# Two moves of panel splits past copies and scalings in a one-core hybrid block on Trainium2

## The reference, cut to what matters

```
proj = h @ w_in                          # all branches' inputs, panels of 256 columns
o_sb  = stick_breaking_attention(q, k, v)              # 8 heads of 64
o_nsa = gate0 * attend(q, compressed keys)             # 15 blocks of 32 tokens, stride 16
      + gate1 * attend(q, selected keys) + gate2 * attend(q, window keys)
o_hg  = hgrn2_recurrence(silu(hg_q), log f, 1 - f, hg_i)   # 4 heads of 128, then a norm and a gate
m = sigmoid(g0) * (o_sb @ w_sb) + sigmoid(g1) * (o_nsa @ w_nsa) + sigmoid(g2) * (o_hg @ w_hg)
x = x + m @ w_out
```

## Time and profile before

| | |
|---|---|
| three runs | 1978.54, 1979.7 (median), 1980.26 us |
| profiled execution | 1978.61 us, span 1976.9 us |
| busy | TensorE 91%, VectorE 67%, ScalarE 41%, GpSimd 21% of the span |
| mean granted TensorE clock | 0.967 of full speed (full is 2.4 GHz, half is 1.2 GHz) |

### The profile page before, as it was taken

One profiled execution on the slowest core, in us unless ns is written; L12 is line 12 of the kernel. 1 busy time (PEld: TensorE's weight loads), 2 busy tenths in 40 slices (PEclk: granted clock), 3 DMA queues, 4 the chain that ended last, 5 costly groups with the idle time before them and its releaser, 6 DMA issues.

```text
span 1976.9 us, 28258 instructions
## 1 busy us (share of the span) xinstructions
PE 1802.3 (91%) x9902; PEld 1375.9 (70%) x9902; DVE 1315.5 (67%) x2522; ACT 812.9 (41%) x1375; POOL 414.7 (21%) x535
## 2 busy tenths in 40 slices
PE   7999899987877787878989999999999999999998
PEld 7988798632333333323378889988889888888887
DVE  5567656867777777777665566765565655776555
ACT  4466343222223212222254444454455544665443
POOL 4000000565456545565310000000000000010000
PEclk9999899998989899998999999999999999999999
DMA  9425374999999999999966554646655656435552
GB/s 243 131 86 150 87 189 141 392 422 422 422 422 422 421 421 422 422 422 422 421 212 199 188 194 160 207 166 191 191 171 181 194 191 211 150 121 171 187 188 98
DMA packets 224244, 496.67 MB, mean 251 GB/s; under 512 B 21653, under 2 KB 170278, under 8 KB 191398
## 3 DMA queue, kind: packets, MB, share of 16 engines
q1 hardware_dynamic: 181264, 221.36, 35.6%
q0 software_dynamic: 38224, 273.04, 33.5%
q10 hardware_dynamic: 4678, 1.21, 0.3%
HBM read 494.53 MB, written 1.05 MB: 251 GB/s over the span
## 4 chain that ended last, share of the span: by engine, by line
PE 67%; DMA 13%; DVE 8%; issue 4%; POOL 3%; ACT 3%; DVEq 0%; POOLq 0%; ACTq 0%
PE ps L2257 39%; PE acc L2257 26%; DMA rows_x<-in_peer_uv,idx_now 6%; DMA arena<-in_peer_uv,idx_now 6%; DVE lo L1440 1%; DMA rows_lo<-in_peer_uv,idx_now 1%; POOL rows L747 1%; ACT hi L817 1%; DVE x L2063 1%; DVE spare_lo L1957 1%; POOL rows_lo L747 1%; POOL rstd L655 0%; ACT xboth L1152 0%; ACT spare_hi L1158 0%; POOL idx_now L740 0%
## 5 line engine op out<-in xcount | busy, mean ns | idle before, releaser
L1440 DVE TENSOR_TENSOR lo<-raw,hi 128x2048 fp32r<-128x2048 f32 x198 | 451.3, 2282 | 193.8 <-ACT hi L817 193.8
L2257 PE MATMUL ps<-xboth,hi 128*128 128x512 f32 (+2 forms) x2400 | 537.0, 344 | 2.1 <-DVE xboth L1461 2.1
L2257 PEld LDWEIGHTS ps<-xboth,hi 128*128 128x128 f32 (+1 forms) x2400 | 409.2, 191 | 47.0 <-issue 4.5
L817 ACT ACTIVATE hi<-raw 128x2048 fp32r<-128x2048 f32 x198 | 376.3, 1902 | 16.3 <-PE acc L2257 9.0
L2257 PE MATMUL ps<-xboth,lo 128*128 128x256 f32 x1840 | 338.3, 283 | 0.0
L2257 PEld LDWEIGHTS ps<-xboth,lo 128*128 128x128 f32 x1840 | 283.0, 191 | 12.6
L650 POOL TENSOR_SCALAR ss<-ss 128x1 f32<-128x1 f32 x26 | 8.9, 342 | 937.8 <-ACT arena L1220 826.1
L2257 PE MATMUL acc<-arena,diag 128*128 128x512 f32 x384 | 175.5, 602 | 8.2 <-ACT diag L1128 7.5
L2257 PE MATMUL acc<-rows,diag 128*128 128x512 f32 x192 | 113.1, 751 | 74.1 <-ACT diag L1128 62.5
L2257 PEld LDWEIGHTS acc<-arena,diag 128*128 128x128 f32 x384 | 72.8, 192 | 105.0 <-issue 85.8
L2257 PEld LDWEIGHTS acc<-rows,diag 128*128 128x128 f32 x192 | 45.1, 243 | 141.2 <-issue 128.1
(11 more groups left out here) (429 smaller groups left out, 2976.5 us busy)
## 6 DMA issues: line engine op xcount, KB each, us to landing
raw<-in_w_ffn_gate SPq DMA_DIRECT2D x44, 1024.0 KB, 5.3
raw<-in_w_ffn_down SPq DMA_DIRECT2D x44, 1024.0 KB, 5.1
raw<-in_w_ffn_up SPq DMA_DIRECT2D x41, 1024.0 KB, 5.3
raw<-in_w_in SPq DMA_DIRECT2D x29, 1024.0 KB, 5.5
raw<-in_w_conv_in SPq DMA_DIRECT2D x11, 1024.0 KB, 5.2
raw<-in_w_kv SPq DMA_DIRECT2D x6, 1024.0 KB, 5.4
raw<-in_w_out SPq DMA_DIRECT2D x4, 1024.0 KB, 5.3
raw<-in_w_conv_out SPq DMA_DIRECT2D x4, 1024.0 KB, 6.7
```

The source lines that it names most:

```text
L817: nc.scalar.activation(hi[s][:, 0:WORDS[p]], raw[s][:, 0:WORDS[p]], ACT.Copy).then_inc(hi_done, 1)
L1440: v.tensor_tensor(lo[s][:, 0:WORDS[p]], raw[s][:, 0:WORDS[p]], hi[s][:, 0:WORDS[p]].bitcast(F32), ALU.subtract).then_inc(lo_done, 1)
L2257: return nc.tensor.matmul(out, l, r, start=first, stop=last)
```

## The change

Two moves; no instruction is added or removed. In compressed attention the split of panel p + 3 = 16 + 2i goes from the end of pair i into pair i + 1 (there it is p + 1), behind that pair's scaling, for i = 0 to 2. VectorE's low halves follow in the same way. In the recurrence ScalarE's two splits of each round go ahead of the two score copies; VectorE's order there stays.

More of the change, by code:

```diff
@@ L995, in nsa_pair @@
                 p = h0 + 1 + 2 * i
+                if i:
+                    split(p + 1)
                 split(p + 2)
@@ L1006, in nsa_pair @@
                     nsa_exp(2 * i + 3, 1)
-                    split(p + 3)
                     nsa_out(i)
@@ L1031, in hg_pair @@
                     gate_evac(m0 + 2)
+                split(m0 + 4 + 2 * j)
+                split(m0 + 5 + 2 * j)
                 for a in range(2):
@@ L1035, in hg_pair @@
                     nc.scalar.activation(large_a[a], ACC[:, 3, 0:3 * P], ACT.Copy).then_inc(h_cross, 1)
-                split(m0 + 4 + 2 * j)
                 if not j:
                     gate_evac(m0 + 3)
-                split(m0 + 5 + 2 * j)
                 for a in range(2):
```

## The result

The changed kernel took 1964.4 us (median of 6 runs, 1962.9 to 1966.1) against 1979.0 (1977.6 to 1980.3, 6 runs): ratio 0.9927, 95% interval 0.9914 to 0.994, 14.6 us less.

The account below looks back on a forecast made before the run. TensorE's standing still was taken to bound the kernel: 3.15 us from attention plus 6.6 from the recurrence (9.9 without a stop) gave 9.75 us less, 1969.3 us written between two bases; range 1965.0 to 1973.2.

Parts of the forecast that it names:

- What bounds the kernel: Whole kernel: TensorE (PE) carries two thirds of what ended last; gains by branch panel 25 carry through one for one.
- Part 1, 3.15 us: Compressed attention: PE's three waits for VectorE's scaling, 3.2 us, go; 0.05 is taken off for lateness in pair 3.
- The tie in pair 3: Attention, pair 3: panel 20's low half and panel 19's evacuation ready at 173.0, just when PE wants them; 0 to 0.4 lost.
- Part 2, the moves: Recurrence: high halves fill ScalarE's idle 9.32 us, VectorE's low halves start 8.0 us earlier; 9.9 us won without a stop.
- round 1's wait for panel 24: Recurrence, round 1: panel 27's high half waits until PE has used panel 24, score copies behind it; covered, 2.9 against 1.9 us.
- Part 2, the 3.3 us taken off: Recurrence, round 1: PE runs out of instructions in the first large scores, then half clock; gain 6.6 instead of 9.9 us.
- Rival 1: Recurrence, round 1: no stop for instructions, store perhaps filled further; 3.15 + 9.9 = 13.05 us, time 1965.6; chance 0.20.
- The price of a stop: Recurrence: behind a stop PE's clock is at half, 16 matmuls in 3.3 us in round 0; panel 25 forecast at full clock.

## Why the prediction was right and wrong

**What bounds the kernel: right.** Each microsecond that PE gained by panel 25 was there at the end, but for 1.2 in the first profile (13.67, 12.49) and 0 in the second.

**Part 1, 3.15 us: right as a term, incomplete as a price.** The three waits went and nothing took their place: 3.27 and 3.28 by the ledger. The tie in pair 3 cost nothing visible (the panel's first matmul is 1.05 behind the transposes' start, with no wait noted). The time of this part alone was 6.0. The clock behind the longest wait, at 2.4 GHz in the one profile that I had, fell to 1.2 in four of the six profiles with that wait; that this makes up most of the other 2.7 is an estimate, with no experiment on the clock behind it. The earlier trace rows show a 1.96 us wait; its price in other executions wasn't asked for.

**Part 2, the moves: right.** Halves into the idle time, low halves behind the masks: VectorE's last level came at 214.54 instead of 227.52; less 1.59 of start-up and 3.27 of attention that is 8.1, forecast 8.0. That round 1's wait for panel 24 is covered was right too: round 0's move alone brings as much as both.

**Part 2, the 3.3 us taken off: wrong.** This is the step that failed. That blocks arrive too slowly for such a burst is right, and with the edge 48 instructions earlier there was a stop. The place was wrong. The prediction took the packet at 229.45 for the moment at which PE stood at the edge, and so put the edge into the first large scores. By the count PE passed that edge in the run before only at 231.0, in the second large scores, and the packet that served it was the one at 221.86: round 0's stop ends with the packet at 196.86, and round 1's edge is three blocks on. So the sum had PE at the edge 2.4 us behind the start of the small scores and the block there at 4.5; in the recurrence-only kernel it is 4.2 and 4.3 to 4.4. The 3.3 us became 0.

How close it was, the repeated changed kernel shows. PE's first load behind the edge starts at 217.0. The block's packet, in the DMA view of 214.0 to 214.1,

```profile
q8 instruction: 1, 0.02, 89.7%
```

starts at 214.03 and takes 1.44 us (89.7% of 16 engines' 0.1 us); with the 1.4 to 1.5 us of every stop the block is there at an estimated 216.9 to 217.0: just in time. Round 0's move alone gives 222.5 for PE and 222.3 to 222.4 for the block, the first profile of the changed kernel 217.0 and 215.7. With the recurrence alone it is 224.2 and 224.3 to 224.4, and no stop is seen, so the estimate holds to some 0.2 us, and in three of the four profiles the margin is no larger. Rival 1's reason, a store filled further, isn't what the runs show: the edge lies later. A packet's time says little of PE's place, since it is fetched ahead: this block's packet starts 0.9 to 1.3 us after PE has passed the edge one block earlier (eleven profiles, those in which the small scores are in one piece), and in the run before, where PE had waits to sit out, it reached the edge 9 us after the packet's start.

**What no term had.** In round 0 PE gained 6.79 - 4.86 = 1.9 (the stop 0.55 shorter, the clock up behind it). VectorE did not gain that, so in the first profile PE waited 0.96 for levels 7 and 8 and then ran 3.4 us at half clock in round 1; against the repeat these cost 0.8 and 1.5 (PE's stretch from branch 24 to panel 25 gained 4.97 here, 7.28 there). Together: 9.9 + 1.9 - 1.0 - 1.5 - 0.3 (the scores' stretch, 4.92 measured, 4.65 in the sum) = 9.0; measured 8.8.

**The sum.** Rival 1, no stop, was the case that came: 1965.6, 1.2 us from the median. That it came so near is partly luck: what no term had, gains of about 1.0 and 1.9 and losses of 1.0, 1.5 and 0.3, nearly cancels. In place of 3.15 + 6.6 the runs have 3.3 + about 1.0 for the clock behind pair 3 + 8.8 to 10.3 for the recurrence: 13.1 to 14.6, measured 14.6 (11.9 to 17.0 by the interval). The range failed because its low end was this rival with half a microsecond of room, and nothing for the clock that goes with waits. The price of a stop was too low as well: where one came, the half clock behind it lasted 6.8 us and not 3.3.

## What to carry to other kernels

A packet of instructions in the DMA view tells when a block was fetched, not where its engine stood: to know whether a burst will meet the edge, count instructions from a stop that a trace shows, or shift the program by a few dozen cheap ones and look. When a wait of two microseconds on PE goes, price the clock behind it too, and look at more than one execution, since one may show it and the next not. And a stop that lies beside another engine's chain is worth nothing until that chain is shorter: three kernels without it were no faster.

## What the hardware showed that was not expected

- A burst of 382 PE instructions in 1.85 us outran the instruction blocks in round 0 of every kernel that kept it whole (stops of 1.9 to 2.7 us, eleven profiles); where half a panel lay between two parts of it, no stop came. PE went on 1.4 to 1.5 us after the end of the 16 KB packet in all twelve stops, and the two stops of one kernel lie 3 x 256 instructions apart. With the fetch's start at 0.9 to 1.3 us and packets of 0.9 to 1.4, an estimate is that 256 instructions of TensorE that pass in less than about 3.2 to 4.2 us run dry at the next edge.
- One and the same kernel, three profiles: the clock behind the 1.96 us wait stayed at 2.4 GHz once and fell to 1.2 twice, for 3.4 us, at a cost of 1.5. In round 1, it stayed up in the profiles whose waits there came to 0.6 and 0.75 us, and fell with 1.6 (3.4 us long), with 3.0 (3.4) and with 2.9 (6.8); with GpSimd's products, 3.2 over both rounds, it fell behind round 0's (1.1 and 0.8; 3.4 us from 199.7 on) and stayed up in round 1.
- A VectorE product of 0.42 us took 2.63 beside a GpSimd product of 2.66.
- Start-up before 30 us differs between executions of one kernel by up to 1.2 us (before, three profiles); it goes with the moment at which the clock goes up to stay: 22.1 us in the first, 20.8 in the other two, and 19.6 in both profiles of the changed kernel. What sets that moment is open.
